# Mixture-of-experts rounds: the down product and both turns move inside the next gate/up product

## The reference, cut to what matters

```python
scores = sigmoid(t @ w_router)              # top 8 of 64 experts per token
def expert_block(tok, g, e):                # up to 128 rows of one expert
    xb = t_pad[tok]                         # gather rows, width 1024
    hid = silu(xb @ w_gate[e]) * (xb @ w_up[e])   # 1024 -> 256, twice
    return (hid @ w_down[e]) * g            # 256 -> 1024
routed = segment_sum(...)                   # 8 rows a token, weighted
return rmsnorm(h + routed + shared(t), g_final)
```

## Time and profile before

| what | value |
|---|---|
| time, median of 3 runs | 1100.18 us (1099.93 to 1103.25) |
| profiled execution, own time | 1100.53 us |
| its span, first to last instruction | 1098.6 us |
| TensorE busy over the span | 1061.5 us (97%) |
| DMA mean over the span | 272 GB/s |
| rounds, first gate/up to last down | about 523 to 1057 us |

### The profile page before, as it was taken

The page is one execution under the profiler, slowest core; times in us unless marked ns, Lnnn a source line. Parts: engine busy times, 40 slices in busy tenths (PEclk is TensorE's granted clock), DMA queues, the critical chain, the costliest instruction groups (busy, mean ns, idle before and its releaser), DMA issues.

```text
span 1098.6 us, 13155 instructions
## 1 busy us (share of the span) xinstructions
PE 1061.5 (97%) x5083; PEld 514.5 (47%) x5083; DVE 388.3 (35%) x885; ACT 229.2 (21%) x490; POOL 122.6 (11%) x186
## 2 busy tenths in 40 slices
PE   7999999989999999999999999999999998999996
PEld 4444688764454584444444433333344333443332
DVE  1897564653220141179222112112211211112157
ACT  4221423653120150051011111111111110111142
POOL 3000000000000000001211211221122111221110
PEclk9999999999999999999999999999999998999998
DMA  7325253321272401247899999999999999999997
GB/s 224 117 77 115 60 166 86 118 77 39 77 305 77 191 17 44 71 197 286 301 418 420 420 420 421 421 419 421 420 420 420 421 420 421 421 420 420 382 414 294
DMA packets 77486, 298.80 MB, mean 272 GB/s; under 512 B 20486, under 2 KB 23851, under 8 KB 50795
## 3 DMA queue, kind: packets, MB, share of 16 engines
q1 hardware_dynamic: 64528, 264.29, 61.4%
q0 software_dynamic: 12672, 33.57, 7.8%
q10 hardware_dynamic: 218, 0.04, 0.0%
HBM read 280.04 MB, written 27.39 MB: 280 GB/s over the span
## 4 chain that ended last, share of the span: by engine, by line
PE 88%; DMA 5%; DVE 2%; ACT 2%; issue 1%; SPq 1%; POOL 0%; DVEq 0%; POOLq 0%; ACTq 0%
PE ps L786 29%; PE ps L1249 26%; PE ps L1266 13%; PE ps L1199 4%; DMA ring<-in_w_down 3%; PE ps L925 3%; PE ps L938 3%; DMA ring<-expert_rows 1%; PE ps L1276 1%; PE ps L1215 1%; PE ps L767 1%; PE ps L974 1%; PE ps L1080 1%; PE ps L1099 1%; DMA expert_rows<-z,ixb 1%
## 5 line engine op out<-in xcount | busy, mean ns | idle before, releaser
L1249 PE MATMUL ps<-ring,z 128*64 128x512 f32 (+2 forms) x832 | 233.2, 594 | 0.9 <-issue 0.9
L786 PE MATMUL ps<-dw,act_t 128*128 128x512 f32 x448 | 194.7, 593 | 0.0
L1266 PE MATMUL ps<-ring,act_t 128*32 128x512 f32 (+2 forms) x512 | 144.0, 606 | 5.4 <-issue 4.6
L786 PEld LDWEIGHTS ps<-dw,act_t 128*128 128x128 f32 x448 | 84.3, 190 | 102.9 <-issue 102.4
L1249 PEld LDWEIGHTS ps<-ring,z 128*64 128x64 f32 (+2 forms) x832 | 74.2, 134 | 94.5 <-issue 92.6
L2459 POOL DMA_INDIRECT expert_rows<-z,ixb x44 | 45.2, 1028 | 392.8 <-ACT z L1626 392.8
L1626 ACT ACTIVATE z<-ps 128x1024 f32<-128x1024 f32 x44 | 45.1, 1025 | 191.4 <-PE ps L1266 191.4
L1630 ACT ACTIVATE tok<-ps 128x256 f32<-128x256 f32 x44 | 16.9, 384 | 296.5 <-PE ps L1249 296.5
L1249 PE MATMUL ps<-dw,z 128*32 128x512 f32 (+2 forms) x272 | 77.8, 594 | 0.0
L1249 PE MATMUL ps<-z 128*32 128x512 f32 (+2 forms) x272 | 77.7, 594 | 0.0
L1249 PE MATMUL ps<-tok,z 128*32 128x512 f32 (+2 forms) x224 | 70.7, 594 | 0.0
(11 more groups left out here) (340 smaller groups left out, 1277.3 us busy)
## 6 DMA issues: line engine op xcount, KB each, us to landing
ring<-in_w_down SPq DMA_DIRECT2D x40, 1024.0 KB, 28.0
ring<-in_w_gate SPq DMA_DIRECT2D x35, 1024.0 KB, 22.5
ring<-in_w_up SPq DMA_DIRECT2D x35, 1024.0 KB, 26.3
act_t<-in_w_down SPq DMA_DIRECT2D x12, 1024.0 KB
dw<-in_w_down SPq DMA_DIRECT2D x12, 1024.0 KB, 23.8
ring<-expert_rows SPq DMA_DIRECT2D x12, 1024.0 KB, 11.2
z<-in_w_gate SPq DMA_DIRECT2D x10, 1024.0 KB
z<-in_w_up SPq DMA_DIRECT2D x10, 1024.0 KB
```

The lines of the kernel that those rows point to most:

```text
L786: ins = pe.matmul(ps[0:m, bank0 + j, 0:n], lhs(w, q * 4 + c4, c4, j), rhs(w, q * 4 + c4, c4, j), start=(q == 0 and c4 == 0), stop=(q == le ...
L1249: ins = pe.matmul(ps[rows, 2 + r % 2, :], xtt[r % 2][:, c, rows], ring_wgu(GU_BUF[x])[:, :, c, :], start=(c == 0), stop=(c == NC_D - 1))
L1266: ins = pe.matmul(ps[rows, 5 + n, :], htt[r % 2][:, c, rows], ring_wd(DN_BUF[x])[:, c, n * 512:(n + 1) * 512], start=(c == 0), stop=(c == 1))
```

## The change: where the down product and the turns stand

On TensorE, round r (from 1 on) now reads: chunks 0 and 1 of gate/up r, turn of hidden r-1, chunks 2 and 3, down r-1, turn of tokens r+1, chunks 4 to 7. ACT takes the down product of r-1 out before the silu of r, not after it. DVE scales the turned tokens of r+2 and works out a gate column after the copy of hidden r, where the tokens of r+1 stood ahead of it. SP's and POOL's programs are not edited.

```diff
@@ round_gate_up (TensorE) @@
             for c in range(NC_D):
+                if r and c == 2:
+                    turn_hidden(r - 1)
+                if r and c == 4:
+                    round_down(r - 1)
+                    if r + 1 < NR:
+                        turn_tokens(r + 1)
                 for rows, x in column_tiles(r):
@@ the loop over rounds (TensorE) @@
-        for r in range(NR):
+        round_gate_up(0)
+        turn_tokens(1)
+        for r in range(1, NR):
             round_gate_up(r)
-            if r + 1 < NR:
-                turn_tokens(r + 1)
-            if r:
-                round_down(r - 1)
-            turn_hidden(r)
+        turn_hidden(NR - 1)
         round_down(NR - 1)
@@ moe_round (ScalarE) @@
         def moe_round(r):
+            if r:
+                down_out(r - 1, (r - 1) % 4)
             act.wait_ge(e_gu, r + 1)
             act.activation(slu[r % 2], ps[:, 2 + r % 2, 0:DE], ACT.Silu).then_inc(e_si, 1)
-            if r:
-                down_out(r - 1, (r - 1) % 4)
@@ moe_round (VectorE) @@
             mul(hid[r % 2], slu[r % 2], ps[:, 2 + r % 2, DE:2 * DE]).then_inc(e_hid, 1)
-            if r + 1 < NR:
-                turned_slots(r + 1)
-                round_gates(r + 1)
+            if r == 0:
+                turned_slots(1)
             dve.wait_ge(e_ht, r + 1)
             dve.tensor_copy(htt[r % 2], ps[:, 4, 0:DE].rearrange("p (c n) -> p c n", c=2)).then_inc(e_hte, 1)
+            if r + 2 < NR:
+                turned_slots(r + 2)
+            if r + 1 < NR:
+                round_gates(r + 1)
```

## The result

The changed kernel takes **1109.41 us** (median of 4 runs, 1108.23 to 1110.53) against 1100.06 us for the kernel before in the same comparison (4 runs, 1099.86 to 1103.25): a ratio of 1.0076, with a 95% interval of 1.0064 to 1.0088. The forecast of 1103.5 had the direction and not the size; the time lies outside its range. The profiled execution took 1110.53 us with a span of 1108.7 us, 10.1 more than before.

A forecast was written before the change was run, and what follows sets the result against it. Bound by weights at the DMA engines' pace up to 929.0, then TensorE's work. Moved work, widths, seams and queue less 2.52 end gate/up 43 7.84 later, the kernel 3.3 later: 1103.8, against the median 1103.5; range 1101.0 to 1107.5.

The forecast's parts named there:

- What bounds the kernel: In the rounds: weights at the DMA engines' pace up to 929.0, then TensorE's work; no wait on DVE or ACT.
- Widths: TensorE's tile changes between neighbouring rounds: 0.35 us per full/narrow pair (14 neighbours), 0.28 per 64/32 pair (20 neighbours).
- seams: Two extra cuts in TensorE's work each round without a width change, taken as 0.04 us a round.
- Loads: SP issues loads later, by 5.1 us; gate and up loads have 8.6 of queue, down loads 2.5.
- the queue may run dry: DMA queue in the first rounds, behind late down loads: 0 to 2.6 us lost, 1.0 taken.
- The clock: At down 32 a wait of 0.8, too short to cost the clock, saves 2.52 us; no wait at down 21.
- the 930.0 of the sum: Start of down 32: weights land at 929.0 plus the queue's 1.0; 1.0 us later than before.
- Cover for the moved turns: In the rounds, hidden rows' 1.0 us after gate/up fits under two chunks, 1.72; other moved work is covered; nothing costs.
- The tail: Behind gate/up 43: last hidden rows uncovered, 5.85 us to the last evacuation; right-half sum starts 5.35 later, at 1064.54.
- some 2 us are absorbed: In the tail, of 5.35 us of delay some 2 are absorbed by waits for rows; DVE goes on 3.3 later.
- The starving queue: Rival: late issues idle the DMA engines 5 us in early rounds, down 32 waits 4.8, clock lost; 1110.0; chance 0.07.

The follow-up runs named there:

- Experiment 6: Kernel before, with SP issuing down loads ahead of gate and up loads at r = 19 and 30 only: 1100.34 us, ratio 0.9996.
- Experiment 1: Kernel before, with SP's gate and up loads also waiting for the down product of round r-1: 1104.71 us, ratio 1.0037.
- experiment 2: Changed kernel, with rounds 0 to 8 in the old order: 1105.67 us, ratio 1.0047 to the kernel before.
- experiment 3: Changed kernel, with SP issuing down loads ahead of gate and up loads: 1105.02 us, ratio 1.0041 to the kernel before.
- Experiment 4: Changed kernel, with VectorE's branch right behind the copy of hidden 41, ahead of scaling the tokens of round 43: 1106.49 us, ratio 1.0056 to the kernel before.
- Experiment 7: Changed kernel, with rounds 42 and 43 in the old order: 1107.22 us, ratio 1.0058 to the kernel before.

## Why the prediction was wrong, point by point

**What bounds the kernel: right.** No wait on ACT or DVE stood inside a round before the change, and none came between round 1 and round 41. Experiment 6 adds what the prediction had only half said: it took TensorE's work to lead to the end from 929.0 on, but reaching the end of it 9 us sooner gained 1.4 in the span, since the rows behind the last weights wait for the DMA engines too.

**Widths: right, seams too dear.** Full-width rounds side by side take 5.15 + 0.23 + 1.72 + 3.43 + 0.89 = 11.42, with the earlier trace rows 6.87 + 0.88 + 3.44 + 0.23 = 11.42 as well: a seam costs 0.00, not 0.02, some 1.7 us too much over 42 rounds. A change between full and narrow costs 5.30 - 5.15 = 0.15 in and 3.63 - 3.43 = 0.20 out, the 0.35 of the forecast. A change between 64 and 32, for which no row had a price, costs 5.44 - 5.30 = 0.14 and 3.57 - 3.43 = 0.14, the value that was taken. From the end of down 21 to the start of down 32 the same work took 129.45 us by the chain, 126.53 before: the widths cost 2.92, where 1.75 + 1.12 = 2.87 was forecast beside the seams. TensorE was ready for down 21 at 795.40, forecast 795.70. These prices agree with the Trainium skill's rule that a switch of the tiling mode drains the engine (TensorEngine Tiling (Array Packing), Key Properties), for 64 against 32 too.

**Loads: the step that failed.** The prediction took 1.0 us for "the queue may run dry", within bounds of 0 to 2.6, from the shortest flight of one down load, once, and called the gate and up loads covered. Measured, the DMA engines moved 3.2 us' worth of bytes less, in several dips from 540 to 575, and down 21's weights came 5.10 late. Two things were wrong in the working. It priced a single load, but each of the first rounds issues late. And it took a flight less 2.5 us for queue, so that 8.6 us of queue were to cover the delay of 5.1. The gate load that the changed kernel issues at 545.53, when the engines moved 168 GB/s (545 to 546), still took 7.1 us to land, and the shortest of all gate and up loads there 4.7:

```profile
DMA to landing us min/median/max: 4.7/15.2/27.1
```

By the 7.1, of the 11.1 in the earlier trace rows some 4.0 us were queue (an estimate), less than the delay. Experiments 1 to 3 show the mechanism: the late issue alone costs it, the first nine rounds hold it, and another order of issue takes it away. Its size at down 21 is only partly explained. Experiments 4 and 7 have the same order in rounds 1 to 41 and the same list of loads, and in their profiled executions the same weights landed 4.0 and 2.3 us late, after early losses of 3.0 and 3.5 us' worth of bytes. So the lateness differs by 2.8 us from execution to execution and does not follow those losses; what makes up the difference stays open.

**The clock: the saving was right, a new loss was missed.** The prediction saved 2.52 at down 32, and that was so. But it had no wait at down 21; there the wait of 3.87 cost 5.35 - 3.65 = 1.70. Both together put down 32 at 924.35 + 5.10 + 1.70 + 2.92 = 934.07, as measured, 4.07 later than the 930.0 of the sum.

**Cover for the moved turns: right in the rounds, one step missing.** Two chunks did cover every turn up to hidden 41. VectorE's branch was not in the working at all: the prediction followed each of VectorE's tensor instructions and not the control flow between them, and the change took its cover away (2.37 us). Experiment 4 shows it.

**The tail: right.** From the end of gate/up 43 (1063.50) to the right-half sum (1071.03) it is 7.53, forecast 7.55; the sum runs without a gap. Its start is 11.84 later than the earlier trace rows, and the span 10.1: the forecast that some 2 us are absorbed holds (1.7). The whole miss is in the two terms above: 4.07 + 2.37 = 6.44 of the 1071.03 - 1064.54 = 6.49.

**The rivals.** The starving queue (1110.0) came nearest in time and in kind: idle DMA engines in the early rounds and a clock lost to the wait behind them. It had the wait at down 32, where it fell at down 21, and it too lacked the branch: that its time is so near is in part luck.

## What to carry to other kernels

When an edit delays the instruction that issues transfers, look at the stretch where the queue is shortest, here the first rounds, price every late issue there, and do not take a load's flight for the queue ahead of it; then try another order of issue before another order of work. When work is moved against the end of an engine's list, follow that engine's branches and register reads as well as its tensor instructions. And where the DMA engines are busy without a gap, as here, look whether time won on the compute engine only comes back as a later wait.

## What the hardware showed that was not expected

The length of the last wait does not tell by itself whether the clock falls. Behind waits of 3.54, 3.87, 4.39 and 4.65 us it fell to its lower level for some microseconds; behind waits of 1.48, 1.57 and 2.87 it stayed. But in experiment 3 it fell in the last down product (0.71 from 1060 to 1065, above), though TensorE had waited only 1.66, 0.94 and 0.72 us since 1045; experiment 2 shows the same. In the changed kernel the waits at the same place were longer, 2.37, 0.94 and 0.72, and the clock held (1.00 from 1065 to 1070).

A read of a count and a branch on VectorE kept it from its next tensor instruction for 5.93 us, in experiment 3 for 5.22. What the read and the branch take of it, no run shows.
